# Prompt attention stores issued from ScalarE's queue, and the last query-key tile normalised in two halves

## The reference

```python
DILATED_PATTERNS = ((128, 1), (512, 4), (2048, 16))
q = rms_norm(q.reshape(B, T, N_ATTN_HEADS, HEAD_DIM), q_norm_g)
k = rms_norm(k.reshape(B, T, N_ATTN_HEADS, HEAD_DIM), k_norm_g)
...
logits = jnp.einsum('brnqhd,brnkhd->brnhqk', qb, kc) * (HEAD_DIM ** -0.5) + bias
m = jnp.max(logits, axis=-1)
e = jnp.exp(logits - m[..., None])
l = jnp.sum(e, axis=-1)
acc = jnp.einsum('brnhqk,brnkhd->brnqhd', e, vc)     # once per pattern; m, l, acc are kept
```

## Time and profile before

| | us |
|---|---|
| median of 3 runs (lowest, highest) | 2816.71 (2813.59, 2826.51) |
| the profiled execution | 2820.47 |
| its span in the trace | 2818.4 |

### The profile page before, as it was taken

One profiled execution on the slowest core, in us unless ns is written; L12 is line 12 of the kernel. 1 busy time (PEld: TensorE's weight loads), 2 busy tenths in 40 slices (PEclk: granted clock), 3 DMA queues, 4 the chain that ended last, 5 costly groups with the idle time before them and its releaser, 6 DMA issues.

```text
span 2818.4 us, 46357 instructions
## 1 busy us (share of the span) xinstructions
PE 2649.4 (94%) x16346; PEld 2285.6 (81%) x16346; DVE 1753.1 (62%) x4030; ACT 1225.5 (43%) x3143; POOL 1131.4 (40%) x781
## 2 busy tenths in 40 slices
PE   6999989979999777999789999999999999999998
PEld 3688858866556443787689999999999999999998
DVE  3268889968777534787465555556555554655555
ACT  3344314457667523555443334443334343334332
POOL 0000000019886002555454455544455554455553
PEclk7999999989999989999899999999999999999999
DMA  7767437744552687475342224254223325423222
GB/s 277 267 217 238 164 112 251 241 132 143 176 184 76 214 319 272 157 240 168 114 151 76 89 70 146 89 191 141 74 81 123 114 70 194 139 76 105 83 68 79
DMA packets 318370, 431.27 MB, mean 153 GB/s; under 512 B 28266, under 2 KB 247766, under 8 KB 312246
## 3 DMA queue, kind: packets, MB, share of 16 engines
q1 hardware_dynamic: 295466, 337.02, 36.7%
q0 software_dynamic: 5072, 81.05, 8.0%
q10 hardware_dynamic: 17604, 10.24, 1.2%
HBM read 353.72 MB, written 146.65 MB: 178 GB/s over the span
## 4 chain that ended last, share of the span: by engine, by line
PE 41%; DVE 3%; issue 3%; DMA 2%; POOL 1%; ACT 1%; SPq 1%; DVEq 0%; POOLq 0%; ACTq 0%
PE ff_u_ps L3036 14%; PE ff_u_ps L3038 13%; PE ff_u_ps L3037 13%; DMA gluT<-h_d 1%; POOL ff_w_lo L2679 1%; DVE ff_a_lo L2903 1%; DMA out_y_prompt_dram<-ff_x_own 0%; SPq L2602 0%; DVE ff_wT L2893 0%; POOL ff_h_lo L2688 0%; ACT ff_h_hi L2738 0%; DMA ff_x_own<-x_d 0%; ACT ff_w_hi L2729 0%; PE ff_out_ps L3031 0%; DVE ff_x_own L2918 0%
## 5 line engine op out<-in xcount | busy, mean ns | idle before, releaser
L2679 POOL TENSOR_TENSOR ff_w_lo<-gluT,ff_w_hi 128x512 fp32r<-128x512 f32 x342 | 459.6, 1354 | 416.0 <-ACT ff_w_hi L2729 415.9
L3036 PE MATMUL ff_u_ps<-ff_a_hi,ff_w_hi 128*128 128x352 f32 (+1 forms) x1536 | 494.0, 322 | 17.6 <-POOL ff_a_lo L2694 9.2
L3037 PE MATMUL ff_u_ps<-ff_a_lo,ff_w_hi 128*128 128x352 f32 (+1 forms) x1536 | 493.0, 321 | 0.0
L3038 PE MATMUL ff_u_ps<-ff_a_hi,ff_w_lo 128*128 128x352 f32 (+1 forms) x1536 | 492.7, 321 | 0.0
L3036 PE MATMUL ff_u_ps<-ff_h_hi,ff_w_hi 128*128 128x352 f32 (+1 forms) x1368 | 442.0, 323 | 15.5 <-DVE ff_h_lo L2841 7.2
L3038 PE MATMUL ff_u_ps<-ff_h_hi,ff_w_lo 128*128 128x352 f32 (+1 forms) x1368 | 439.5, 321 | 0.0
L3037 PE MATMUL ff_u_ps<-ff_h_lo,ff_w_hi 128*128 128x352 f32 (+1 forms) x1368 | 438.1, 320 | 0.0
L2936 DVE SCALAR_TENSOR_TENSOR ff_y<-ff_u_ps,modT,ff_y 128x352 f32<-128x352 f32 (+2 forms) x336 | 188.1, 570 | 317.4 <-PE ff_u_ps L3038 317.3
L2729 ACT ACTIVATE ff_w_hi<-gluT 128x512 fp32r<-128x512 f32 x342 | 210.5, 626 | 287.8 <-PE ff_u_ps L3038 252.6
L2679 POOL TENSOR_TENSOR ff_w_lo<-ff_wT,ff_w_hi 128x512 fp32r<-128x512 f32 x168 | 225.4, 1343 | 272.6 <-ACT ff_w_hi L2729 172.9
L3036 PEld LDWEIGHTS ff_u_ps<-ff_a_hi,ff_w_hi 128*128 128x128 f32 x1536 | 289.8, 189 | 22.2 <-POOL ff_a_lo L2694 10.3
(11 more groups left out here) (347 smaller groups left out, 5137.8 us busy)
## 6 DMA issues: line engine op xcount, KB each, us to landing
gluT<-in_w_ff_dram SPq DMA_DIRECT2D x192, 512.0 KB, 5.0
out_new_k_sample_dram<-in_cache_k_dram POOLq DMA_DIRECT2D x8, 4088.0 KB, 16.1
out_new_v_sample_dram<-in_cache_v_dram POOLq DMA_DIRECT2D x8, 4088.0 KB, 16.5
dwq<-in_w_ada_dram SPq DMA_DIRECT2D x32, 512.0 KB, 8.7
gluT<-in_cache_k_dram SPq DMA_DIRECT2D x16, 1024.0 KB, 11.1
sa_vn<-in_cache_v_dram SPq DMA_DIRECT2D x16, 1024.0 KB, 19.3
gluT<-h_d SPq DMA_DIRECT2D x80, 176.0 KB, 4.2
mx_acc<-acc_d SPq DMA_DIRECT2D x16, 768.0 KB, 8.2
```

The costliest lines, as they stand in the source:

```text
L2679: pool.tensor_tensor(slot_view(w_lo, s), src, slot_view(w_hi, s).bitcast(F32), ALU.subtract).then_inc(w_lod, 1)
L3036: pe.matmul(out, w_hi[:, s % WR, w], hi, start=first, stop=False, skip_group_check=more)
L3037: pe.matmul(out, w_hi[:, s % WR, w], lo, start=False, stop=False, skip_group_check=more)
L3038: return pe.matmul(out, w_lo[:, s % WR, w], hi, start=False, stop=last, skip_group_check=more)
```

## The change

ScalarE issues the stores of the half patterns on its own queue: store_half(ch) stands at the top of its loop two iterations after the one in which VectorE makes the eighth copy. SyncE's list keeps the loads, dw_d, the key loads and the statistics. In the projection the last tile's chain is taken in two halves (squares, norms, scaling, transposes), tile 14's transposes move between the two halves of tile 16's products, and SyncE stores tiles 14 and 15 before the last keys.

```diff
@@ -1171,9 +1171,10 @@
                                 sp.dma_start(dst, src).then_inc(first_in, 16)
                         sp.wait_ge(dw_done, 1)
                         sp.dma_start(dw_d[:, :, SEQ:TOK], dwS[:]).then_inc(dw_out, 16)
+                        store_t(NT - 2)
+                        store_t(NT - 1)
                         store_k(NT)
-                        for u in range(NT - 2, NT + 1):
-                            store_t(u)
+                        store_t(NT)
                         sp.wait_ge(dw_out, 16)
                         sp.wait_ge(k_out[0], 16 * 9)
                         sp.wait_ge(k_out[1], 16 * 8)
@@ -1189,7 +1190,7 @@
 
                     @block.scalar
                     def _(act):
-                        def turned(u):
+                        def turned_queries(u):
                             n = rows_of(tile_at[u])
                             if u >= 2:
                                 act.wait_ge(t_out[u % 2], t_stored(u))
@@ -1201,27 +1202,34 @@
                             act.activation(qkT[:, u % 2, 0, c0:4, 0:n], t_ps[:, 0, c0:4, 0:n], ACT.Copy, scale=qgain[:, 0:1])
                             if c0:
                                 act.activation(first_q[:, i * P:(i + 1) * P], t_ps[:, 0, 0], ACT.Copy, scale=qgain[:, 0:1])
+
+                        def turned_keys(u):
+                            n = rows_of(tile_at[u])
+                            i = tile_at[u]
+                            c0 = int(i < NT)
                             act.wait_ge(t_pe, 2 * u + 2)
                             if c0:
                                 act.activation(first_k[:, i * P:(i + 1) * P], t_ps[:, 1, 0], ACT.Copy)
                             act.activation(qkT[:, u % 2, 1, c0:4, 0:n], t_ps[:, 1, c0:4, 0:n], ACT.Copy).then_inc(t_done, 1)
 
+                        def square(u, half):
+                            n = rows_of(tile_at[u])
+                            if u >= 1 and half == 0:
+                                act.wait_ge(red_done, u)
+                            act.wait_ge(z_pe, 2 * u + half + 1)
+                            return act.activation(sqr[0:n, half * AW:(half + 1) * AW], z_ps[(2 * u + half) % 6][0:n], ACT.Square)
+
                         def squares(u):
+                            square(u, 0)
+                            square(u, 1).then_inc(sqr_done, 1)
+
+                        def scaled(u, heads=range(2 * H)):
                             n = rows_of(tile_at[u])
-                            if u >= 1:
-                                act.wait_ge(red_done, u)
-                            for half in range(2):
-                                act.wait_ge(z_pe, 2 * u + half + 1)
-                                ins = act.activation(sqr[0:n, half * AW:(half + 1) * AW], z_ps[(2 * u + half) % 6][0:n], ACT.Square)
-                            ins.then_inc(sqr_done, 1)
-
-                        def scaled(u):
-                            n = rows_of(tile_at[u])
-                            act.wait_ge(rs_done, u + 1)
+                            act.wait_ge(rs_done, u + 1 + heads.start // H)
                             if u >= 2:
                                 act.wait_ge(t_pe, 2 * (u - 1))
                                 act.wait_ge(k_out[u % 2], k_stored(u - 2))
-                            for h in range(2 * H):
+                            for h in heads:
                                 z = z_ps[(2 * u + h // H) % 6][0:n, h % H * DH:(h % H + 1) * DH]
                                 ins = act.activation(nrm[0:n, u % 2, h * DH:(h + 1) * DH], z, ACT.Copy, scale=rsq[0:n, u % 2, h:h + 1])
                             ins.then_inc(z_free, 1)
@@ -1231,12 +1239,21 @@
                             act.activation(w_hi[:, k], w_ring4[:, k % 4], ACT.Copy).then_inc(w_hid, 1)
                         squares(0)
                         for u in range(NT + 1):
-                            scaled(u)
-                            if u + 1 <= NT:
+                            if u < NT:
+                                scaled(u)
+                            else:
+                                square(NT, 1).then_inc(sqr_done, 1)
+                                scaled(NT, range(H))
+                            if u + 1 < NT:
                                 squares(u + 1)
+                            if u + 1 == NT:
+                                square(NT, 0).then_inc(sqr_done, 1)
                             if u >= 1:
-                                turned(u - 1)
-                        turned(NT)
+                                turned_queries(u - 1)
+                                turned_keys(u - 1)
+                        turned_queries(NT)
+                        scaled(NT, range(H, 2 * H))
+                        turned_keys(NT)
 
                     @block.vector
                     def _(v):
@@ -1254,9 +1271,21 @@
                             rsqrt(v, step, rsq[0:n, u % 2], ssq[0:n], tmp[0:n])
                             v.sem_inc(rs_done, 1)
 
+                        def half_norms(half):
+
+                            heads = slice(half * H, (half + 1) * H)
+                            v.wait_ge(sqr_done, NT + 1 + half)
+                            v.tensor_reduce(ssq[:, heads], sqr[:, half * AW:(half + 1) * AW].rearrange("p (h d) -> p h d", d=DH), AX.X, ALU.add).then_inc(red_done, 1)
+                            v.wait_ge(red_done, NT + 1 + half)
+                            step(v.tensor_scalar(ssq[:, heads], ssq[:, heads], 1.0 / DH, EPS, ALU.mult, ALU.add))
+                            if half == 0:
+                                v.wait_ge(z_free, NT - 1)
+                            rsqrt(v, step, rsq[:, NT % 2, heads], ssq[:, heads], tmp[:, heads])
+                            v.sem_inc(rs_done, 1)
+
                         def key_gain(u):
                             n = rows_of(tile_at[u])
-                            v.wait_ge(z_free, u + 1)
+                            v.wait_ge(z_free, u + 1 + u // NT)
                             k_rows = nrm[0:n, u % 2, AW:].rearrange("p (h d) -> p h d", d=DH)
                             v.tensor_tensor(k_rows, k_rows, kgain[0:n].unsqueeze(1).to_broadcast([n, H, DH]), ALU.mult).then_inc(nrm_done, 1)
 
@@ -1276,7 +1305,11 @@
                                 step(v.tensor_tensor(dwS[:], dwS[:], dwT[:], ALU.add))
                         v.sem_inc(dw_done, 1)
                         for u in range(NT + 1):
-                            head_norms(u)
+                            if u < NT:
+                                head_norms(u)
+                            else:
+                                half_norms(0)
+                                half_norms(1)
                             for o in range(QK_OPS * u // (NT - 1), QK_OPS * min(u + 1, NT - 1) // (NT - 1)):
                                 late_op(v, cstep, o)
                             key_gain(u)
@@ -1284,11 +1317,11 @@
 
                     @block.tensor
                     def _(pe):
-                        def products(u):
+                        def products(u, columns=range(2)):
                             n = rows_of(tile_at[u])
                             if u >= 2:
                                 pe.wait_ge(h_ld[u % HB], 32 * ((u - 2) // HB + 1))
-                            for c in range(2):
+                            for c in columns:
                                 if u >= 3 and c == 0:
                                     pe.wait_ge(z_free, u - 2)
                                 z = z_ps[(2 * u + c) % 6][0:n, :]
@@ -1304,18 +1337,27 @@
 
                         def turn_qk(u):
                             n = rows_of(tile_at[u])
-                            pe.wait_ge(nrm_done, u + 1)
+                            if u < NT:
+                                pe.wait_ge(nrm_done, u + 1)
                             if u >= 1:
                                 pe.wait_ge(t_done, u)
                             for half in range(2):
+                                if u == NT:
+                                    if half == 0:
+                                        pe.wait_ge(z_free, NT + 1)
+                                    else:
+                                        pe.wait_ge(nrm_done, NT + 1)
                                 for c in range(4):
                                     mm = pe.transpose(t_ps[:, half, c, 0:n], nrm[0:n, u % 2, (4 * half + c) * P:(4 * half + c + 1) * P], ident[0:n, 0:n])
                                 mm.then_inc(t_pe, 1)
 
-                        for u in range(NT + 1):
+                        for u in range(NT):
                             products(u)
                             if u >= 2:
                                 turn_qk(u - 2)
+                        products(NT, (0,))
+                        turn_qk(NT - 2)
+                        products(NT, (1,))
                         turn_qk(NT - 1)
                         turn_qk(NT)
 
```

(15 more changed lines are left out.)

## The result

The changed kernel's median is 2833.99 us (10 runs, 2826.74 to 2840.26), that of the kernel before 2819.77 us (10 runs on the same chip): a ratio of 1.0044 (95% interval 1.003 to 1.0058). 2811.0 was forecast, in 2800 to 2822. The profiled execution is the fastest of the ten, 2826.74 us, with a span of 2824.6.

A forecast was written before the change was run, and what follows sets the result against it. It found no single bounding engine: the attention loop runs in lockstep, with VectorE waiting 18.4 us for stores. Terms summed to -5.7 from the profiled 2820.5, giving 2814.8, or 2811.0 against the median; range 2800 to 2822.

The forecast's parts named there:

- Stall in pair 1: Attention pair 1: VectorE's wait for the acc_d store shrinks to 0.2 us once ScalarE issues it; -4.5 us.
- Stall in pair 2: Attention pair 2: VectorE's wait for the store goes, as it no longer stands behind SyncE's loads; -8.4 us.
- The issues on ScalarE: Attention loop: store issues ahead of pa_oT partly delay ScalarE and so TensorE; +5.0 us, between 0 and +14.
- Stall in pair 3: Attention pair 3: the store still starves behind two cache copies, with SyncE's other transfers taking turns; +0.5 us.
- A new stall in pair 0: Attention pair 0: the later store falls behind the cache copy, so VectorE waits 2 to 3 us; +3.0 us.
- the issues are free and pair 0 escapes: Attention stage: store gets through before pair 0's copy and ScalarE's issues hide; about 2802 us, chance 0.16.
- The projection's tail: Projection's last tile: halving its chain and storing tile 14 earlier ends ScalarE's last copies sooner; -1.0 us.
- The stalls stay: Attention pairs 1 and 2: store packets come no earlier on their own queue; sum +7.2, 2823.9 us, chance 0.11.
- ScalarE's issue is blocked: Attention pairs 1 and 2: ScalarE's issues stick as SyncE's did, stopping TensorE too; +23.9, 2840.6 us, chance 0.08.
- nothing hides: Attention loop: all 31 store issues on ScalarE cost full price, +9 more; 2820 us, chance 0.05.

The follow-up runs named there:

- e3: The changed kernel run again for a second profile, against the kernel before: 2829.48 us, ratio 1.001.
- e4: The kernel before, run again unchanged: 2824.19 us, ratio 0.999.
- e10: The kernel before with VectorE's query copies written as tensor_scalar with a running sum: 2814.63 us, ratio 0.9977 to the kernel before.
- e9: The changed kernel with VectorE's query copies written as tensor_scalar with a running sum: 2805.87 us, ratio 0.9942 to the kernel before.
- e5: The kernel before without GpSimd's 40 convolution pairs (multiplication, addition) in the attention stage: 2813.04 us, ratio 0.9965 to the kernel before.
- e6: The changed kernel without GpSimd's 40 convolution pairs in the attention stage: 2799.18 us, ratio 0.9917 to the kernel before.
- e11: e9 with one cache copy moved from the attention stage's last pair into the projection: 2794.4 us, ratio 0.99 to the kernel before.
- e12: The kernel before with only one cache copy moved from the attention stage's last pair into the projection: 2807.05 us, ratio 0.995.
- e1: The kernel before with only the attention's stores moved to ScalarE, projection tail as before: 2830.68 us, ratio 1.0016.
- e8: The changed kernel with cache copies asked for in rows of 1792 bytes (packets stayed 65 KB): 2829.39 us, ratio 1.0019 to the kernel before.
- e2: The kernel before with only the projection's tail in halves, stores still on SyncE: 2822.48 us, ratio 0.9987.
- e7: The kernel before with cache copies asked for in rows of 1792 bytes (packets stayed 65 KB): 2820.71 us, ratio 0.9989.

## Why the prediction was wrong

**The failed step.** "Stall in pair 1" and "Stall in pair 2" took what the stall cost (-4.5 and -8.4) to be what the pair would save. Both stalls went, by the mechanism that was given (q10 shares the turns with q1; the store of pair 1 landed at 745.4 where 746.4 was forecast), but pair 1 became 3.4 us longer and pair 2 only 5.0 us shorter: -1.6 together in place of -12.9. The step that was missing is the one after the gain: what stands where the loop now arrives? The stall had held two query copies, in half patterns 8 and 14, away from an addition of GpSimd's. Without it they stand 0.12 us inside and are held for its whole length. "The issues on ScalarE" failed in the same way: they were priced as a delay, and their 0.28 us in number 9 pushed a third copy from just ahead of an addition to just behind its start, which cost 3.3 us. TensorE paused for 2.2 us behind each of the three and its clock fell to half, for 3.4 or 6.8 us in the first profile and for 30.7 behind one of them in e3's. The trace of before had query copies of up to 2.06 us, five times the usual, and they were not looked at.

The -8.4 for pair 2 was also read from a single execution. 4.5 us of it are the stall; the rest lies in number 14 (18.9 us), where a query copy was held for 1.91 us. In e4, the same program with a stall of 3.6 us there, number 14 takes 14.9 us and pair 2 is 3.7 us longer than pair 0, not 8.4.

**The same terms with the wait gone.** Against e10, e9 saves 5.3 us in pair 1 and 7.2 in pair 2 (87.8 to 82.6, 89.5 to 82.3); forecast were 4.5 and 8.4. Here these two terms held within 1.2 us. The whole is 8.8 us by the medians (13.9 in e5 and e6) where the sum gave 5.7, with the terms below off in both directions.

**Stall in pair 3.** +0.5 forecast. The wait went from 10.4 to 11.1 and the half pattern from 25.1 to 25.8: +0.7. The cause was the two cache copies, as e11 and e12 show.

**A new stall in pair 0.** +3.0 forecast, 0 in the changed kernel, e1 and e3 (number 1 at 15.0), but 1.2 to 2.1 us of waiting in e6, e8, e9 and e11 (number 1 at 16.7 to 17.0). The mechanism was right; which of the two issues comes first differs between executions, so that the changed kernel escaped was luck. I had put the store at 649, after the copy's 648.65; it comes at 647.25, the copy at 647.92, and 990 of its packets go through in 647 to 650, before the first of the copy. In e9 the copy's packets come first and VectorE waits 1.8 us at 659.7. Queue q10 in 647 to 650 of the changed kernel:

```profile
q10 hardware_dynamic: 990, 0.51, 59.5%
```

**The issues on ScalarE.** +5.0 forecast, 1.2 to 1.8 measured as a delay (their part in number 9 is told above). ScalarE's sequencer takes the DMA while two or three ACTIVATEs are still ahead of the place where it stands in the list:

```profile
677.08 0.37 ACTq L1683 DMA_DIRECT2D acc_d<-pa_o_sb  x1
677.15 0.49 ACT L1699 ACTIVATE pa_score<-pa_score,pa_stat 128x256 f32<-128x256 f32 x1
677.48 0.54 ACTq L1683 DMA_DIRECT2D acc_d<-pa_o_sb  x1
677.55 0.19 ACT L1699 ACTIVATION_READ_ACCUMULATOR pa_score<-pa_score,pa_stat 128x1 f32 x1
677.64 0.57 ACT L1702 ACTIVATE pa_probT<-pa_t_ps 128x512 f32<-128x512 f32 x1
678.12 0.28 ACT L1692 ACTIVATE pa_oT<-pa_oT_ps 128x128 f32<-128x128 f32 x1
```

Two issues, 0.94 us together, and pa_oT starts without a gap. In pattern 2, where the work ahead of it is shorter, something shows:

```profile
690.77 0.53 ACTq L1683 DMA_DIRECT2D acc_d<-pa_o_sb  x1
690.86 0.36 ACT L1702 ACTIVATE pa_probT<-pa_t_ps 128x256 f32<-128x256 f32 x1
691.41 0.28 ACT L1692 ACTIVATE pa_oT<-pa_oT_ps 128x128 f32<-128x128 f32 x1 [0.19 <-issue]
```

Half patterns 4, 10, 16 and 22 are 11.1 us against 10.8: 4 x 0.3 = 1.2 us. Between e5 and e6, where no copy is held, numbers 9 and 21 are 0.3 us longer too, which makes 1.8. The rival "the issues are free and pair 0 escapes" had this part right.

**The projection's tail.** -1.0 forecast. ScalarE's last copies:

```profile
612.96 0.58 ACT L1202 ACTIVATE qk_qkT<-qk_t_ps,qk_qgain 128x384 f32<-128x384 f32 x1 [1.27 <-PE qk_t_ps L1351]
...
613.68 1.74 ACT L1234 ACTIVATE qk_nrm<-qk_z_ps,qk_rsq 128x64 f32<-128x64 f32 x8
...
617.36 0.28 ACT L1212 ACTIVATE first_k<-qk_t_ps 128x128 f32<-128x128 f32 x1 [1.93 <-PE qk_t_ps L1351]
617.53 0.48 ACT L1213 ACTIVATE qk_qkT<-qk_t_ps 128x384 f32<-128x384 f32 x1
```

They end at 618.0, and as everything from the projection on is shifted by 0.9 us (its first product comes at 400.2 and not 399.3), that is 0.9 earlier; from the first product to the first scores it is 221.8 us in place of 223.4. Over all kept profiles this is 221.4 to 221.8 in the seven kernels with the new tail and 222.7 to 224.3 in the seven without: about 1.8 us, more than the 1.0 forecast. The second heads' scaling stands behind the first half's copies (613.44 to 613.68), as forecast.

**The rivals.** "The stalls stay" is excluded by the wait rows, "ScalarE's issue is blocked" by the issues of at most 0.54 us, "nothing hides" by the row at 678.12. None of the four was the one that came. The blocked case's 2840.6 lies nearest to the measured 2834.0, by luck: no issue was blocked. Its sum was also wrong. It is -5.7 + 29.6, which keeps the gain of 12.9 that it says is lost; without that gain it would be +36.8.

**What stays open.** The three comparisons give 1.0044, 1.001 and 1.0019. The first one's ten runs, 2826.7 to 2840.3, lie about where e3's seven slower ones do (2828.0 to 2841.4); its 14 us are not accounted for. The long stretch of low clock is in e3's profile alone of the four that kernels with plain copies and stores on ScalarE have, and what parts the two groups of runs stays open. Why the clock comes back after 3.4 us in one execution and after 30.7 in another was not tried. The MLP's 4.6 us go with short windows of half clock, and may not be chance: it takes 1445.6 to 1448.1 us in those four profiles and 1443.3 to 1445.4 in the five with plain copies, additions and stores on SyncE (before, e2, e4, e7, e12), though its instructions are the same. No experiment was aimed at it. That the clock fell because of TensorE's pause is read from the order of events, and e6 and e9, with neither in pairs 1 and 2, agree; it wasn't tried alone.

## What to carry to other kernels

When a stall is taken away, ask not only what it cost but what stands where the loop will then arrive. Here two engines were let go by the same scores, and the stall was what had kept their instructions apart; a delay of 0.28 us did the same damage at another place. Look in the profile for one kind of instruction whose longest is several times its median, before the change and after; here the kernel before, too, gained 6.9 us when that group was freed (e10). And when several transfers are late behind one large copy, move the copy first: one moved line gave more than a queue of its own for the victims.

## What the runs showed of the hardware

- A VectorE copy of 128x256 fp32 from SBUF to SBUF (0.38 us) that meets a GpSimd addition of two SBUF tensors ends 0.24 to 0.26 us after the addition, in all 20 cases of the two profiles. Under a GpSimd multiplication of one tensor (2.84 us) it was held when it started 0.30 to 0.98 us after the multiplication, and ended 1.34 to 1.42 us after the multiplication's start; from 1.01 us on it kept its 0.35 to 0.40. With a sum written out it takes 0.57 to 0.64 us in e9, 21 times inside an addition.
- Each query copy of 2.38 us or more that started at full clock (15 in six profiles) had TensorE's clock at half within 6 us of its start.
- ScalarE's sequencer issues a DMA while ACTIVATEs ahead of it run: about 1 us of issue (0.37 + 0.54) cost nothing at 677, and 0.19 us at 691.
- A copy from DRAM to DRAM asked for in rows of 1792 bytes moved in packets of 65 KB (47 for 3.07 MB).
